# Placing the operands of a split fp32 matmul at multiples of 2048 bytes of the SBUF row

## The chip, the core and the metric

The kernel runs on one core of a Trainium2 chip. The metric is the device time of one execution in microseconds; lower is better. The engines are named as in the profile: PE (TensorE), PEld (TensorE's weight loads), DVE (VectorE), ACT (ScalarE), POOL (GpSimd) and SP (SyncE, which only issues DMAs here).

## The reference

Two transformer blocks are computed one after the other on a sequence of 512 tokens with a width of 1024, all in float32. Cut to what matters:

```python
def first_block(x, ...):                       # two layers
    for l in range(2):
        z = rms_norm(x, g_mix_norm[l]) @ w_in[l]
        # latent attention of 4 heads | a gating unit | moving averages, each normed and joined
        x = x + mix @ w_out[l]
        h = rms_norm(x, g_ffn_norm[l])
        x = x + (silu(h @ w_gate[l]) * (h @ w_up[l])) @ w_down[l]      # hidden width 2816

def second_block(h, p, ...):                   # two layers
    for i in range(2):
        # layer 0: gated short convolution; layer 1: dilated attention, 3 groups of 8 heads
        h = h + mixer(rmsnorm(h, norm_mix[i]))
        h = h + square(relu(rmsnorm(h, norm_mlp[i]) @ w_up[i])) @ w_down[i]   # hidden width 4096
        h = h + sigmoid(rmsnorm(h, norm_ple[i]) @ w_gate[i]) * (p[i] @ w_proj[i])
    return rmsnorm(h, norm_final)
```

## The kernel before

Activations are kept transposed: the channel is the partition, the 512 tokens lie along the row. The residual is `x_res`, eight tiles of 128 x 512. A product of two float32 matrices is made of three matmuls on a single-pass type (fp32r): each operand is split into a high part, which that type holds exactly, and a low part, the rest, and high x high, high x low and low x high are added up in PSUM. This is `triple`, lines 437 to 441; most of the kernel's matmuls come from its three lines. The exact fp32 matmuls (norm sums, transposes, attention scores and values) don't go through it.

The weights come as 216 slabs of 128 x 2048 floats, in the order in which they are used. SP fetches slab n into one half of `w_stage` as soon as GpSimd has split the slab before it in that half. GpSimd (`split`, lines 376 to 382) writes `w_high` (L379, a rounding copy) and then `w_low` (L381, the subtraction), each with two halves, after TensorE has finished the slab two before. A slab holds 16 blocks of 128 x 128, so 48 matmuls of 512 columns. Where weights are the stationary operand, a block of 512 bytes of the row is loaded and a 2048-byte activation tile is moved through it; for the values of the attentions and for the gating unit the roles are exchanged, and 512 or 256 columns of weights are moved.

The phases are mix, ffn, mix, ffn, conv, mlp, ple, attn, mlp, ple and a last norm (`ORDER`). At the start of each, ScalarE writes `x_high` from the residual (L970) and VectorE `x_low` (L1280). The hidden activations of ffn and mlp are split in the same manner: ScalarE writes the high part, VectorE the low one (L1322, L1343), and `down` (L515 to L544) moves them. In the mlp, VectorE scales a tile out of PSUM (L1337), squares it (L1340) and makes the low part (L1343).

All tensors of a partition's row are allotted one after the other, in the order of the `sb(...)` calls from L164 on, each rounded up to 32 bytes. Ahead of them lie the scratch for DMA descriptors, 16,384 bytes unless the program asks for less, and 128 bytes more. From this the places follow:

| tensors | bytes | first byte, past a multiple of 2048 |
|---|---|---|
| `x_res`, `x_high`, `x_low` | 16,384 each | 128 |
| `w_stage`, `w_high`, `w_low` | 16,384 each | 128 |
| `rstd`, `rope` | 2,048 and 4,096 | 128 |
| `ident`, `ones`, `cols_sb`, `stat` | 512, 512, 608, 96 | 128, 640, 1152, 1760 |
| `shared_area` (`ffn_*`, `mlp_*`, `ple_*`, `lat_*`, `mla_*`, `gate_pool_*`, `attn_*`, `qk*`, `v_tok*`) | 90,112 | 1856 |
| `work_area` (`work`, `scores2`, `probs_t2`) | 16,384 | 1856 |

Within the shared area every tensor that `triple` reads is a whole number of tiles of 2048 bytes, so all their tiles lie 1856 bytes past a multiple. In the mix phase `pool_in`, of 4,224 bytes, stands in the middle of the area, and `mla_out`, `pool_out`, `probs_t1` and `w_spat` lie behind it, 1984 past. Weight blocks begin every 512 bytes from 128 on, slices of 256 columns every 1024.

Of the kernel before, what the change touches and what calls it, by code (L numbers as in the profile page):

```python
# [24 lines left out]
F32 = mybir.dt.float32  # L25
# [7 lines left out]
P = 128  # L33
T = 512
# [12 lines left out]
EPS = 1e-6  # L47
MASKED = -1e30
TOK = T // P

COLUMNS = [("mix_norm", 16), ("ffn_norm", 16), ("q_lat", 4), ("kv_lat", 2), ("q_head", 2), ("k_head", 2),
# [4 lines left out]
N_COLUMNS = sum(n for _, n in COLUMNS)  # L57
# [40 lines left out]
SPLITS_MIX = 3 + DT  # L98
MIX_STEPS, MIX_HEADS, MIX_VALUES = 2 * HEADS * TOK, 2 * HEADS, 2 * HEADS
MIX_LOADS, FIRST_LOADS = 10, 2  # L100
# [52 lines left out]
def build(nc, a):  # L153

    ctx = ExitStack()
    with ctx:
        def sb(name, shape, dt=F32, stack=ctx):
            return stack.enter_context(nc.sbuf_tensor(name, shape, dt))
# [2 lines left out]
            return ctx.enter_context(nc.semaphore(name))  # L161

        x = sb("x_res", [P, DT, T])  # L164
        xh = sb("x_high", [P, DT, T], F32R)
        xl = sb("x_low", [P, DT, T], F32R)
        stage = sb("w_stage", [P, 2, SLAB])
        wh = sb("w_high", [P, 2, SLAB], F32R)
        wl = sb("w_low", [P, 2, SLAB], F32R)
        rstd = sb("rstd", [P, T])  # L170
        rope = sb("rope", [P, 2, T])
        ident = sb("ident", [P, P])
        ones = sb("ones", [P, P])
        cols = sb("cols_sb", [P, N_COLUMNS])
        stat = sb("stat", [P, 24])

        with ExitStack() as s:
            hh1 = sb("ffn_high", [P, FFN_TILES, T], F32R, s)
            hl1 = sb("ffn_low", [P, FFN_TILES, T], F32R, s)  # L180
# [6 lines left out]
        with ExitStack() as s:  # L187
            qk1 = sb("qk1", [P, 2 * HEADS, T], F32, s)
            vt1 = sb("v_tok1", [P, TOK, HEADS * V_HEAD], F32, s)
            lath = sb("lat_high", [P, 3, T], F32R, s)  # L190
            latl = sb("lat_low", [P, 3, T], F32R, s)
            kr = sb("k_rope", [P, T], F32, s)
            kr_positions = kr[:].bitcast(I32)
            vs = sb("sgu_v", [P, TOK, 256], F32, s)
            u = sb("sgu_u", [P, 2, T], F32, s)
            pin = sb("pool_in", [P, 2, 16 + T], F32, s)
            o1 = sb("mla_out", [P, HEADS, T], F32, s)
            po = sb("pool_out", [P, 2, T], F32, s)
            pt1 = sb("probs_t1", [P, TOK, T], F32, s)
            spat = sb("w_spat", [P, 4, P], F32, s)  # L200
            tri = sb("tri_sb", [P, P], F32, s)
            bsp = sb("b_spat", [P, 2, P], F32, s)
            gsv = sb("g_sgu", [P, 256], F32, s)
            wpool = sb("w_pool_sb", [P, 2, 64], F32, s)
            inv = sb("inv_count_sb", [P, 2, T], F32, s)
            diag = sb("diag_sb", [P, T], F32, s)
            pa = sb("window_a", [P, T + 16], F32, s)
            pb = sb("window_b", [P, T + 16], F32, s)
            nar = sb("token_cols", [P, 232], F32, s)
            areas = [nar]  # L210
        with ExitStack() as s:
            qk2 = sb("qk2", [P, 2 * GROUPS * BATCH_HEADS, T], F32, s)
            v2 = sb("v_tok2", [P, GROUPS, TOK, T], F32, s)
            o2 = sb("attn_out", [P, GHEADS, T], F32, s)
        with ExitStack() as s:

            mha = sb("mla_high", [P, HEADS, T], F32R, s)
            mla_ = sb("mla_low", [P, HEADS, T], F32R, s)
            sb("under_v_tok1", [P, TOK, HEADS * V_HEAD], F32, s)
            mhb = sb("gate_pool_high", [P, 4, T], F32R, s)  # L220
# [1603 lines left out]
```

## Time and profile before

| | |
|---|---|
| timed runs | 2793.62, 2794.19 and 2796.15 us; median 2794.19 |
| span of the profiled execution, first to last instruction | 2791.8 us |
| PE, share of the span with a matmul in flight | 95% |
| PEld, DVE, ACT, POOL | 77%, 54%, 17%, 53% |
| bytes moved by DMA | 236.70 MB, 85 GB/s over the span |
| slabs: DMAs of 1 MB each | 216 |

The profile gives no time of its own for the profiled execution beside its span; the span is 2.4 us below the median of the timed runs.
### The profile page before, as it was taken

The page shows a single profiled execution, that of the slowest core. Times are in us where ns is not written, and L with a number is a line of the kernel's source. Part 1 is how long each engine was busy: PE and PEld are TensorE (multiplying, and loading weights), DVE is VectorE, ACT ScalarE, POOL GpSimd, SP SyncE. Part 2 cuts the span into 40 slices and gives each one's busy share as a digit, 9 for nine tenths or more (in the row PEclk, how much of TensorE's full clock was granted, in tenths as well). Part 3 has the DMA queues.
Part 4 walks back from the last instruction along what each step waited for, and adds up shares of the span by engine and source line. Part 5 has one row for each costly group of instructions (what it writes and reads, how often), then busy time and mean ns, then how long its engine had stood idle before and what let it go on. Part 6 is the DMA issues. An engine that isn't in the chain of part 4 may idle for free.

```text
span 2791.8 us, 30840 instructions
## 1 busy us (share of the span) xinstructions
PE 2656.8 (95%) x11906; PEld 2156.5 (77%) x11906; DVE 1505.0 (54%) x1678; ACT 471.4 (17%) x777; POOL 1475.1 (53%) x465
## 2 busy tenths in 40 slices
PE   6889999999899999999999999898999999999997
PEld 6668888877588888787878887687788877878875
DVE  5766554047575440456751715895379357805526
ACT  3342111023421110101100102200310042100012
POOL 4526656544266665555655665455336514656652
PEclk9899999999899999999999999999999999999998
DMA  4102222231022322222322222222112302222221
GB/s 147 61 31 91 91 104 90 92 110 61 2 104 92 104 90 93 88 102 84 109 76 103 91 91 99 76 102 78 61 46 90 106 31 83 91 85 96 91 93 58
DMA packets 36891, 236.70 MB, mean 85 GB/s; under 512 B 4048, under 2 KB 5584, under 8 KB 9168
## 3 DMA queue, kind: packets, MB, share of 16 engines
q1 hardware_dynamic: 33456, 230.78, 24.0%
q10 hardware_dynamic: 3360, 4.85, 0.5%
q8 instruction: 56, 0.92, 0.1%
q14 instruction: 19, 0.16, 0.0%
HBM read 233.51 MB, written 2.10 MB: 84 GB/s over the span
## 4 chain that ended last, share of the span: by engine, by line
PE 82%; DVE 11%; issue 3%; ACT 2%; DMA 1%; POOL 0%; DVEq 0%; ACTq 0%; SPq 0%; POOLq 0%
PE psum L439 25%; PE psum L440 25%; PE psum L441 25%; DVE work L1340 3%; PE psum L887 2%; DVE work L1264 2%; DVE x_low L1280 1%; PE psum L871 1%; PE psum L649 1%; DVE work L1337 1%; PE psum L896 1%; ACT mlp_high L998 1%; DVE x_res L1384 1%; PE psum L759 1%; PE psum L775 1%
## 5 line engine op out<-in xcount | busy, mean ns | idle before, releaser
L379 POOL TENSOR_SCALAR w_high<-w_stage 128x2048 fp32r<-128x2048 f32 x216 | 418.5, 1937 | 1261.5 <-PE psum L441 1249.3
L381 POOL TENSOR_TENSOR w_low<-w_stage,w_high 128x2048 fp32r<-128x2048 f32 x216 | 1026.1, 4751 | 18.0
L439 PE MATMUL psum<-x_high,w_high 128*128 128x512 f32 x2048 | 807.3, 394 | 38.5 <-DVE x_low L1280 36.9
L440 PE MATMUL psum<-x_low,w_high 128*128 128x512 f32 x2048 | 801.0, 391 | 0.0
L441 PE MATMUL psum<-x_high,w_low 128*128 128x512 f32 x2048 | 800.8, 391 | 0.0
L439 PEld LDWEIGHTS psum<-x_high,w_high 128*128 128x128 f32 x2048 | 387.2, 189 | 123.9 <-issue 31.8
L440 PEld LDWEIGHTS psum<-x_low,w_high 128*128 128x128 f32 x2048 | 387.2, 189 | 82.9 <-issue 2.4
L441 PEld LDWEIGHTS psum<-x_high,w_low 128*128 128x128 f32 x2048 | 386.9, 189 | 81.3
L1304 DVE TENSOR_TENSOR x_res<-psum,x_res 128x512 f32<-128x512 f32 x64 | 47.0, 735 | 387.0 <-PE psum L441 387.0
L439 PE MATMUL psum<-mlp_high,w_high 128*128 (+1 forms) x576 | 230.2, 400 | 13.7 <-DVE work L1337 10.8
L440 PE MATMUL psum<-mlp_low,w_high 128*128 (+1 forms) x576 | 229.5, 398 | 0.0
L441 PE MATMUL psum<-mlp_high,w_low 128*128 (+1 forms) x576 | 229.4, 398 | 0.0
L970 ACT ACTIVATE x_high<-x_res,cols_sb 128x512 fp32r<-128x512 f32 x80 | 61.1, 771 | 545.1 <-DVE x_res L1304 545.1
L1343 DVE TENSOR_TENSOR mlp_low<-work,mlp_high 128x512 f32 x64 | 115.2, 1800 | 59.3 <-ACT mlp_high L998 59.3
L439 PEld LDWEIGHTS psum<-mlp_high,w_high 128*128 128x128 f32 x576 | 109.4, 190 | 42.5 <-DVE work L1337 12.6
L439 PE MATMUL psum<-ffn_high,w_high 128*128 (+1 forms) x352 | 138.7, 394 | 0.0
L440 PE MATMUL psum<-ffn_low,w_high 128*128 (+1 forms) x352 | 138.7, 394 | 0.0
L441 PE MATMUL psum<-ffn_high,w_low 128*128 (+1 forms) x352 | 138.7, 394 | 0.0
L1264 DVE TENSOR_TENSOR work<-work 128x512 f32<-128x512 f32 x87 | 134.2, 1543 | 2.6 <-ACT work L932 1.4
L1623 DVE TENSOR_TENSOR qk<-work 32x512 f32 x48 | 131.4, 2738 | 1.7
L441 PEld LDWEIGHTS psum<-mlp_high,w_low 128*128 128x128 f32 x576 | 109.3, 190 | 26.9
L440 PEld LDWEIGHTS psum<-mlp_low,w_high 128*128 128x128 f32 x576 | 109.4, 190 | 26.4
(240 smaller groups left out, 3172.3 us busy)
## 6 DMA issues: line engine op xcount, KB each, us to landing
w_stage<-in_wstream SPq DMA_DIRECT2D x216, 1024.0 KB, 4.9
x_res<-in_x SPq DMA_DIRECT2D x2, 1024.0 KB, 12.1
out_x<-attn_out SPq DMA_DIRECT2D x8, 256.0 KB, 2.1
inv_count_sb<-in_inv_count ACTq DMA_DIRECT2D x2, 512.0 KB, 8.9
ple_proj<-in_p ACTq DMA_DIRECT2D x2, 512.0 KB, 3.7
v_tok<-in_mask ACTq DMA_DIRECT2D x1, 576.0 KB, 3.8
w_spat<-in_spatial ACTq DMA_DIRECT2D x2, 256.0 KB, 5.3
diag_sb<-in_diag ACTq DMA_DIRECT2D x2, 256.0 KB, 9.6
```

Source lines behind the costliest of these rows:

```text
L379: pool.tensor_scalar(wh[:, s, :], stage[:, s, :], 1.0, 1.0, ALU.mult, ALU.mult).then_inc(high_written, 1)
L381: pool.tensor_tensor(wl[:, s, :], stage[:, s, :], wh[:, s, :].bitcast(F32), ALU.subtract) \
L439: pe.matmul(out, wa, ra, start=start, stop=False)
L440: pe.matmul(out, wa, rb, start=False, stop=False)
L441: return pe.matmul(out, wb, ra, start=False, stop=stop)
L887: last = pe.matmul(ps[:, b, r * P:(r + 1) * P], v, pt2[:, (n % 2) * 768 + kb * P:(n % 2) * 768 + (kb + 1) * P], start=kb == 0, stop=kb == 5)
L970: act.activation(dst, src, ACT.Copy, scale=gcol(p.gain + m)).then_inc(x_scaled, 1)
L1264: tt(W[:, ACC, :], W[:, ACC, :], src, ALU.add).then_inc(squares_added, 1)
L1304: tt(dst, src, dst, ALU.add).then_inc(drained[m], 1)
L1340: dve.scalar_tensor_tensor(out=W[:, 6 + m, :], in0=W[:, b, :], scalar=0.0, in1=W[:, b, :], op0=ALU.max, op1=ALU.mult).then_inc(product_rea ...
L1343: tt(hl2[:, bass.ds(i * 4 + b, 1), :].rearrange("p a t -> p (a t)"), W[:, 6 + m, :], hh2[:, bass.ds(i * 4 + b, 1), :].rearrange("p a t -> ...
L1623: tt(rotated, W[rows, 2 * m, :], W[rows, 2 * m + 1, :], ALU.add).then_inc(head_ready, 1)
```

## The change

The constants (`ident`, `ones`, `cols_sb`, `stat`) are allotted first, a padding that nobody reads fills up to byte 4096, and `rstd`, `rope`, the residual, its two parts and the slabs follow. The scratch for DMA descriptors is asked for at 1,024 bytes instead of 16,384, which makes room for the padding. As every tensor from there on up to `pool_in` is a whole number of 2048 bytes, the tiles of `x_high`, `x_low`, `w_high`, `w_low` and of the shared and the work area then begin at multiples of 2048, weight blocks at multiples of 512. In the mix phase `pool_in` goes behind the small constants, so that the tensors it pushed off move to multiples as well. No instruction, wait or transfer is added, removed or reordered.

```diff
+SCRATCH = 1024
+ROW_PAD = 4096 - (SCRATCH + 128) - 4 * (2 * P + 152 + 24)
...
+        ident = sb("ident", [P, P])
+        ones = sb("ones", [P, P])
+        cols = sb("cols_sb", [P, N_COLUMNS])
+        stat = sb("stat", [P, 24])
+        sb("up_to_a_row", [P, ROW_PAD // 4])
+        rstd = sb("rstd", [P, T])
+        rope = sb("rope", [P, 2, T])
         x = sb("x_res", [P, DT, T])
         xh = sb("x_high", [P, DT, T], F32R)
         xl = sb("x_low", [P, DT, T], F32R)
         stage = sb("w_stage", [P, 2, SLAB])
         wh = sb("w_high", [P, 2, SLAB], F32R)
         wl = sb("w_low", [P, 2, SLAB], F32R)
-        rstd = sb("rstd", [P, T])
-        rope = sb("rope", [P, 2, T])
-        ident = sb("ident", [P, P])
-        ones = sb("ones", [P, P])
-        cols = sb("cols_sb", [P, N_COLUMNS])
-        stat = sb("stat", [P, 24])
...
-            pin = sb("pool_in", [P, 2, 16 + T], F32, s)
             o1 = sb("mla_out", [P, HEADS, T], F32, s)
             po = sb("pool_out", [P, 2, T], F32, s)
             pt1 = sb("probs_t1", [P, TOK, T], F32, s)
             spat = sb("w_spat", [P, 4, P], F32, s)
+            inv = sb("inv_count_sb", [P, 2, T], F32, s)
+            diag = sb("diag_sb", [P, T], F32, s)
             tri = sb("tri_sb", [P, P], F32, s)
             bsp = sb("b_spat", [P, 2, P], F32, s)
             gsv = sb("g_sgu", [P, 256], F32, s)
             wpool = sb("w_pool_sb", [P, 2, 64], F32, s)
-            inv = sb("inv_count_sb", [P, 2, T], F32, s)
-            diag = sb("diag_sb", [P, T], F32, s)
+            pin = sb("pool_in", [P, 2, 16 + T], F32, s)
...
-    nc = bacc.Bacc("TRN2", target_bir_lowering=False, num_devices=1)
+    nc = bacc.Bacc("TRN2", target_bir_lowering=False, num_devices=1, dynamic_dma_scratch_size=SCRATCH)
```

## Rows read from the trace of the kernel before

**Rows 1.** The page, part 4: the chain that ended last, by engine and by line.

```profile
PE 82%; DVE 11%; issue 3%; ACT 2%; DMA 1%; POOL 0%; DVEq 0%; ACTq 0%; SPq 0%; POOLq 0%
PE psum L439 25%; PE psum L440 25%; PE psum L441 25%; DVE work L1340 3%; PE psum L887 2%; DVE work L1264 2%; DVE x_low L1280 1%; PE psum L871 1%; PE psum L649 1%; DVE work L1337 1%; PE psum L896 1%; ACT mlp_high L998 1%; DVE x_res L1384 1%; PE psum L759 1%; PE psum L775 1%
```

**Rows 2.** Groups by line, L439: out<-moving,stationary, shape, count | busy us, mean ns | idle before.

```profile
L439 PE MATMUL psum<-x_high,w_high 128*128 128x512 f32 x2048 | 807.3, 394 | 38.5 <-DVE x_low L1280 36.9
...
L439 PE MATMUL psum<-mlp_high,w_high 128*128 (+1 forms) x576 | 230.2, 400 | 13.7 <-DVE work L1337 10.8
...
L439 PE MATMUL psum<-ffn_high,w_high 128*128 (+1 forms) x352 | 138.7, 394 | 0.0
...
L439 PE MATMUL psum<-w_high,x_high 128*128 128x512 f32 x192 | 76.1, 396 | 8.8 <-DVE stat L1399 8.8
...
L439 PE MATMUL psum<-gate_pool_high,w_high 128*128 128x512 f32 x64 | 25.8, 404 | 3.1 <-DVE gate_pool_low L1551 3.1
...
L439 PE MATMUL psum<-w_high,x_high 128*128 128x256 f32 x64 | 20.6, 322 | 0.0
```

**Rows 3.** Three stretches: us, busy (count) of PE, PEld, DVE, ACT, POOL, PEclk, DMA.

```profile
300.00:400.00 100.00, 100.00 (x443) 82.80 (x442) 51.30 (x37) 17.81 (x23) 62.13 (x19) 1.00 0.27 94
470.00:570.00 100.00, 100.00 (x431) 80.12 (x430) 0.00 (x0) 0.00 (x0) 58.65 (x18) 1.00 0.27 93
2630.00:2710.00 80.00, 80.00 (x344) 64.11 (x344) 7.16 (x7) 2.80 (x5) 45.76 (x15) 1.00 0.28 93
```

**Rows 4.** Timeline of PE at half clock: start us, us, engine line op; four lie between.

```profile
595.81 0.63 PE L440 MATMUL psum<-x_low,w_high 128*128 128x512 f32 x1
...
597.94 0.63 PE L439 MATMUL psum<-x_high,w_high 128*128 128x512 f32 x1
```

**Rows 5.** Timeline of PE, weights as moving operand, 256 columns; five lie between.

```profile
62.34 0.28 PE L439 MATMUL psum<-w_high,x_high 128*128 128x256 f32 x1
...
63.06 0.28 PE L439 MATMUL psum<-w_high,x_high 128*128 128x256 f32 x1
```

**Rows 6.** Timeline of PE, exact fp32 matmuls of the attention; one row merges like ones.

```profile
2261.77 0.82 PE L896 MATMUL psum<-ident,scores 128*128 128x128 f32 x6
2262.43 1.02 PE L871 MATMUL psum<-qk 128*128 128x512 f32 x2
2263.29 0.38 PE L872 MATMUL psum<-qk 128*128 128x128 f32 x2
```

**Rows 7.** Timeline of two matmuls and their consumers, with the weight loads that follow.

```profile
285.98 0.39 PE L441 MATMUL psum<-x_high,w_low 128*128 128x512 f32 x1
285.98 0.19 PEld L439 LDWEIGHTS psum<-x_high,w_high 128*128 128x128 f32 x1
...
286.41 0.69 DVE L1316 TENSOR_TENSOR work<-psum,rstd 128x512 f32<-128x512 f32 x1 [3.51 <-PE psum L441]
...
1983.02 0.39 PE L441 MATMUL psum<-w_high,x_low 128*128 128x512 f32 x1
1983.45 0.69 ACT L1179 ACTIVATE v_tok<-psum,stat 128x512 f32<-128x512 f32 x1 [2.03 <-PE psum L441]
...
1984.20 0.19 PEld L871 LDWEIGHTS psum<-qk 128*128 128x128 f32 x1 [1.22 <-issue]
```

**Rows 8.** Spans and mean granted TensorE clock of the core.

```profile
core 0: 2791.8 us, clock 0.973
```

**Rows 9.** Timeline of POOL and DVE in an mlp up run, one slab.

```profile
2406.39 1.92 POOL L379 TENSOR_SCALAR w_high<-w_stage 128x2048 fp32r<-128x2048 f32 x1 [3.89 <-PE psum L441]
2408.39 4.92 POOL L381 TENSOR_TENSOR w_low<-w_stage,w_high 128x2048 fp32r<-128x2048 f32 x1
...
2405.30 0.69 DVE L1340 SCALAR_TENSOR_TENSOR work<-work 128x512 f32<-128x512 f32 x1
...
2409.48 4.38 DVE L1340 SCALAR_TENSOR_TENSOR work<-work 128x512 f32<-128x512 f32 x1
```

**Rows 10.** The page, part 6: the slab's DMA, count, size, us from issue to landing.

```profile
w_stage<-in_wstream SPq DMA_DIRECT2D x216, 1024.0 KB, 4.9
```

## Prediction

> **What bounds the kernel now.** The chain that ended last comes first: 82% of it is TensorE, 75% in the three lines of `triple`, and nothing else has over 3% in one line [rows 1]. So the end is set by how often TensorE can start one of these matmuls. The reader should next look at how many there are and of which operands, in the groups by line and shape [rows 2]; each row stands for three lines with equal counts, and `mla_high` and `attn_high` have the same counts as `gate_pool_high`. That makes, of 512 columns, 3 x 2048 with `x_high` and 3 x 192 with weights as the moving operand (6720 together, all moving operands 128 bytes past a multiple of 2048), and 3 x (352 + 576 + 3 x 64) = 3360 whose moving operand lies in the shared area, 1856 bytes past a multiple (the smaller groups there are left out). 3 x 64 = 192 move 256 columns of weights.
>
> A share of the chain doesn't say how far these are from their best, so the next view is the stretches of the long runs, all at the full granted clock [rows 3]. A matmul of 0.39 us touches a stretch if it starts in it or up to 0.39 us before, so the pitch from start to start is 100.39 / 443 = 226.6 ns with `x_high`, and 100.39 / 431 = 232.9 and 80.39 / 344 = 233.7 with `ffn_high` and `mlp_high`; I use 233.3. Two pitches for the same instruction, the same shape and the same clock: what differs is the operand's address.
>
> At half clock five `x_high` matmuls take 597.94 - 595.81 = 2.13 us, 426 ns each [rows 4], and half of this is 213.3 ns (512 columns at 2.4 GHz): the 13.3 ns of `x_high` and the 20.0 ns of the shared area exist at the full rate alone. Six matmuls of 256 columns take 63.06 - 62.34 = 0.72 us, 120 ns each against 106.7: 13.3 ns again, so the extra is paid once for an instruction and not by length [rows 5]. Exact fp32 matmuls, which take their elements at half the rate, hardly pay: six start-to-starts of L896 take 2262.43 - 2261.77 = 0.66 us, 110 ns where two passes of 128 columns are 106.7, and two records of L871 take 0.86 us where four passes of 512 are 0.853 [rows 6], the latter with `qk` from the shared area. Nor is it the weight load that runs beside the matmul: a consumer starts 286.41 - 285.98 = 0.43 us after a matmul with a load beside it and 1983.45 - 1983.02 = 0.43 us after one whose next load comes only at 1984.20 [rows 7].
>
> One rule gives all three numbers: 128 past a multiple of 2048 leaves 128 bytes, 32 elements, to the next multiple of 256; 1856 leaves 192 bytes, 48 elements; and 1024 further on, where every second weight slice of 256 columns starts, leaves 32 again. At 2.4 GHz 32 elements are 13.3 ns and 48 are 20.0 ns: as if the piece up to the next multiple went at half rate. This is inferred from three values; a multiple of 256 itself isn't among them.
>
> The Trainium skill bears on this in two places. The Trainium skill (TensorE: Matmul & The Clock Gate, section "Wait — 56ns, not 53.3ns?") puts back-to-back starts at N columns over 1.2 GHz when cold and at N over 2.4 GHz plus some 2.5 ns when warm, with no word on addresses; the half-clock rows agree, the full-clock rows stand 11 and 17 ns above it, and a change that reached it would end near 2660. The Trainium skill (SBUF — State Buffer, section "Who interferes with whom") holds that TensorE waits on nobody at SBUF; taken for the whole story it leaves the address no part, which is the no-change rival, and the two pitches of rows 3 speak against it.
>
> **The change, part by part.** Its core moves every moving operand of the split products, and every weight block, onto a multiple of 512 or 2048 bytes. No instruction is added or removed and no wait is moved; what changes is the price of 10,272 matmuls. No row shows such a matmul at a multiple at full rate, so its pitch is bounded: from below by 213.3 ns (half of rows 4), from above by 240.0 ns (the same rule with a whole piece of 64 elements, 26.7 ns, at half rate; the third rival below). Between them lie the 226.6 ns of now. I take 213.3 + 3 = 216.3 ns, the 3 ns being what each recorded matmul of L896 shows over its columns; it is nearest because the rule leaves no broken piece at a multiple. Then:
> - 6720 x (226.6 - 216.3) = 69.2 us
> - 3360 x (233.3 - 216.3) = 57.1 us
> - 192 x (120 - 109.7) = 2.0 us
>
> together 128.3 us. Matmuls at half clock gain nothing: the mean granted clock of 0.973 [rows 8] is 5.4% of the span, 151 us, at half; at 0.426 us each that holds at most 350 matmuls, and as much of it is waiting I take 170, so 2 us less.
>
> What hides the other engines. GpSimd splits each slab in 1.92 + 4.92 us and then waits 3.89 us for TensorE [rows 9]; a slab of 48 matmuls goes from 10.88 to 10.38 us, so that wait shrinks to 3.4 and still covers it. VectorE's L1340 takes 0.69 us alone and 4.38 when GpSimd's subtraction holds it [rows 9]; that is 3.7 us of slack in a slab, of which 0.5 goes. A slab's DMA needs 4.9 us [rows 10] of 10.38. If one of these covers were gone, what is missing from 0.5 us would come back on each slab of its stage (64 slabs hold the MLPs: at most 32 us). I take 2 us given back where stages begin and end, since the chain's VectorE part (11%, rows 1) isn't shortened.
>
> The rest costs nothing either way: no DMA is issued by GpSimd (the DMA issues of the page are SP's and ACT's, of which rows 10 show SP's main one), so nobody uses the smaller scratch; the padding is never read; `pool_in` gives up its place to become the odd one and feeds eight fp32 matmuls. The exact fp32 matmuls move too: 3 ns a record less or more on some 1,400 is 4 us, in both directions, taken as nothing. The DMA of a slab lands at another offset with the same 8,192 bytes a partition: nothing by the queue's slack.
>
> Sum: 128 - 2 - 2 = 124 us. The profiled span is 2791.8 us; the median of the timed runs is 2794.2, 2.4 us more, which the change doesn't touch. 2794 - 124 = 2670 us. With 213.3 ns it would be 6720 x 13.3 + 3360 x 20 + 192 x 13.3 = 159 us, 2635.
>
> **The rivals.**
> - Only the shared area gains. The 13.3 ns could belong to any single-pass fp32 matmul at full rate and only the additional 6.7 ns to an address off a multiple of 128 (1856 is, 128 isn't). Then the moved operands all run at 226.6: 3360 x 6.7 = 23 us, 2771. For it: the 256-column slices pay 13.3 too, wherever they start. Against it: the exact match of 32 and 48 elements.
> - The change doesn't do what it says: the pitch follows something else (which tile is read, not where), 2794. Against it: operands of different stages share a pitch when they share an offset.
> - Slower: the first piece of up to 256 bytes always goes at half rate, since the reader only gets ahead after it. Then a multiple is the worst place, 240.0 ns: 6720 x 13.4 + 3360 x 6.7 + 192 x 13.3 = 115 us, 2909. It fits all three values as well as my reading, and decides as soon as the mean pitch exceeds today's 228.8 ns. [...]
> - Part of the gain: a pitch of 218 to 224 ns or a cover that gives way, 2700 to 2760.
>
> **How the numbers follow.** The forecast has 0.50 (2635 to 2700 by its bounds), part of the gain 0.06, only the shared area 0.18, no change 0.12, slower 0.14. A change of 0.2%, 5.6 us, is about the least that a measurement of this kernel can tell from none. The range reaches from 2635 to 2800 and leaves out the slower case. Faster: 0.50 + 0.06 + 0.18 = 0.74; the same 0.12; slower 0.14.
>
> **What would show it.** In the changed profile, a stretch of 100 us of `x_high` should hold 464 matmuls, and so should one of `ffn_high`; 443 in both means the first rival, 418 the slower one. The 256-column matmuls should be 110 ns apart. GpSimd's wait for TensorE should shrink by 0.5 us a slab, VectorE's stay off the path. If the pitch is right and the time isn't, a cover is gone: TensorE would then wait for L381 or for a bank to be drained. The prediction is wrong altogether if the pitch doesn't depend on where the operand begins.

## The result, and the profile after

The changed kernel took 2776.55 us, median of four executions (2771.68, 2771.82, 2781.28 and 2784.05), against 2793.99 for the kernel before beside them: a ratio of 0.9939, 95% interval 0.992 to 0.9958. That is 17 us less, where 124 were forecast. The profiled execution is the one of 2781.28 us, with a span of 2779.5. Lines of the code stand one further down than before (L440 to L442 are `triple`'s).

The chain of the changed kernel, by engine and by line, to be read beside [rows 1]:

```profile
PE 79%; DVE 14%; issue 3%; ACT 2%; DMA 1%; POOL 0%; DVEq 0%; ACTq 0%; SPq 0%; POOLq 0%
PE psum L440 24%; PE psum L441 24%; PE psum L442 24%; DVE work L1341 3%; PE psum L888 2%; DVE work L1265 2%; DVE x_low L1281 1%; PE psum L872 1%; DVE work L1338 1%; PE psum L760 1%; PE psum L897 1%; ACT mlp_high L999 1%; DVE x_res L1385 1%; PE psum L776 1%; DVE qk L1395 1%
```

TensorE's part fell from 82 to 79% and VectorE's rose from 11 to 14%: something was given back there. First the pitch, though. Three stretches at full clock, with `x_high`, `ffn_high` and `mlp_high` as moving operand (length, PE busy and count, granted clock, DMA share, GB/s), answering [rows 3]:

```profile
300.00:400.00 100.00, 100.00 (x443) 1.00 0.27 94
470.00:570.00 100.00, 100.00 (x443) 1.00 0.28 101
2610.00:2690.00 80.00, 80.00 (x355) 1.00 0.30 105
```

The count with `x_high` is 443, as before; that with `ffn_high` went from 431 to 443, and that with `mlp_high` from 344 to 355 in 80 us. So there is now one pitch, 100.39 / 443 = 226.6 ns (80.39 / 355 = 226.5), and it is the lower of the two of before. That the shared area lost 6.7 ns a matmul is worth 3360 x 6.7, some 22 us, and two of the four executions show just that, 2794 - 22 = 2772. The matmuls of 256 columns didn't move either, against [rows 5] (six pitches of 120 ns):

```profile
62.18 0.28 PE L440 MATMUL psum<-w_high,x_high 128*128 128x256 f32 x1
...
62.90 0.28 PE L440 MATMUL psum<-w_high,x_high 128*128 128x256 f32 x1
```

The granted clock is where it was, 0.974 against 0.973 [rows 8], and in the mlp GpSimd still waits for TensorE between two slabs, 3.9 and 4.0 us here against 3.89 [rows 9]; an up run moves `x_high`, whose pitch stayed.

The other two executions are 10 and 12 us longer, and the profiled one, of 2781 us, is one of them. TensorE's waits in its second mixing layer (570 to 765 us) show most of it: what waits, for what, total, times and longest.

```profile
PE psum L789 <- DVE work L1577: 10.4, 4, 5.6
PE psum L722 <- DVE qk L1502: 6.9, 1, 6.9
PE psum L440 <- DVE x_low L1281: 3.7, 1, 3.7
```

The second of these isn't in the trace of the kernel before, whose largest waits there are 10.4 and 3.5 us on the other two lines. The first mixing layer (0 to 190 us) has it too, shorter, and again the kernel before has none there:

```profile
PE psum L722 <- DVE qk L1502: 2.6, 1, 2.6
```

What makes it is the subject of the last experiments.

### The profile page after: what moved, and what is told of

The parts are those of the page before. It is cut to its first block, busy times and chain, and to the rows that moved or that the text cites. A ratio compares the mean times of both kernels' runs of the same rounds, so it can differ in the third digit from the quotient of the medians.

```text
span 2779.5 us, 30840 instructions
## 1 busy us (share of the span) xinstructions
PE 2631.9 (95%) x11906; PEld 2155.3 (78%) x11906; DVE 1508.2 (54%) x1678; ACT 471.7 (17%) x777; POOL 1475.9 (53%) x465
## 3 DMA queue, kind: packets, MB, share of 16 engines
q10 hardware_dynamic: 3360, 4.85, 0.6%
## 4 chain that ended last, share of the span: by engine, by line
PE 79%; DVE 14%; issue 3%; ACT 2%; DMA 1%; POOL 0%; DVEq 0%; ACTq 0%; SPq 0%; POOLq 0%
PE psum L440 24%; PE psum L441 24%; PE psum L442 24%; DVE work L1341 3%; PE psum L888 2%; DVE work L1265 2%; DVE x_low L1281 1%; PE psum L872 1%; DVE work L1338 1%; PE psum L760 1%; PE psum L897 1%; ACT mlp_high L999 1%; DVE x_res L1385 1%; PE psum L776 1%; DVE qk L1395 1%
## 5 line engine op out<-in xcount | busy, mean ns | idle before, releaser
L382 POOL TENSOR_TENSOR w_low<-w_stage,w_high 128x2048 fp32r<-128x2048 f32 x216 | 1026.8, 4754 | 18.0
L440 PE MATMUL psum<-x_high,w_high 128*128 128x512 f32 x2048 | 806.9, 394 | 38.3 <-DVE x_low L1281 36.7
L442 PE MATMUL psum<-x_high,w_low 128*128 128x512 f32 x2048 | 800.1, 391 | 0.0
L440 PEld LDWEIGHTS psum<-x_high,w_high 128*128 128x128 f32 x2048 | 386.7, 189 | 124.5 <-issue 31.4
L442 PEld LDWEIGHTS psum<-x_high,w_low 128*128 128x128 f32 x2048 | 386.6, 189 | 80.4
L440 PE MATMUL psum<-mlp_high,w_high 128*128 (+1 forms) x576 | 227.0, 394 | 14.2 <-DVE work L1338 11.0
L442 PE MATMUL psum<-mlp_high,w_low 128*128 (+1 forms) x576 | 226.0, 392 | 0.0
L440 PEld LDWEIGHTS psum<-mlp_high,w_high 128*128 128x128 f32 x576 | 109.5, 190 | 39.1 <-DVE work L1338 12.7
L440 PE MATMUL psum<-ffn_high,w_high 128*128 (+1 forms) x352 | 136.9, 389 | 0.0
L442 PE MATMUL psum<-ffn_high,w_low 128*128 (+1 forms) x352 | 136.9, 389 | 0.0
L442 PEld LDWEIGHTS psum<-mlp_high,w_low 128*128 128x128 f32 x576 | 109.4, 190 | 23.0
```

What stands on the lines that cost most here:

```text
L382: pool.tensor_tensor(wl[:, s, :], stage[:, s, :], wh[:, s, :].bitcast(F32), ALU.subtract) \
L440: pe.matmul(out, wa, ra, start=start, stop=False)
L442: return pe.matmul(out, wb, ra, start=False, stop=stop)
```

## The experiments

**e1_micro: the pitch by itself.** TensorE alone, every address chosen; 40 matmuls to a line of the code:

```diff
+            for j in range(R): pe.matmul(ps[:, 0, :], st(0, j), mv(0, j), start=j == 0, stop=j == R - 1)
+            for j in range(R): pe.matmul(ps[:, 1, :], st(0, j), mv(64, j), start=j == 0, stop=j == R - 1)
...
+            for j in range(R): pe.matmul(ps[:, 3, :], st(64, j), mv(0, j), start=j == 0, stop=j == R - 1)
...
+            for j in range(R): pe.matmul(ps[:, 1, :], st(64, j), mv(64, j), start=j == 0, stop=j == R - 1)
```

`mv(m, j)` is a tile of the moving operand m bytes past a multiple of 2048, `st(w, j)` a weight block w bytes past one.

> Leaves out the whole computation: one TensorE queue of 41 x 40 matmuls and nothing beside them, one source line for each case, so that the pitch of a case is the distance between two lines' first starts over 40. Cases: moving operand 0 to 1856 bytes past a multiple of 2048 with the weights at 0; weights 32 to 1856 past with the moving operand at 0; both off; 128, 256, 384 and 512 columns; 128, 64 and 32 stationary columns; 64 rows; the same weight block or the same moving tile each time; bf16 and exact fp32. Theory A (multiples of 128: a moving operand off a multiple of 128 bytes costs 6.7 ns, and 13.3 ns belong to any such matmul at full rate): 226.7 ns at 0, 128, 256, 512, 1024; 233.3 at 4, 16, 32, 64, 192, 1856; the weights' address changes nothing. Theory B (the place within 2048 counts by itself): only 0 or a few places give 226.7. Theory C (the weights' address counts, or the two operands' offset against each other): 233.3 with the weights at 64 and the moving operand at 0, and 226.7 again with both at 64. Of the 13.3 ns: if the weight load makes them, 64 or 32 stationary columns or one weight block read again should give less, down to 213.3; if they belong to the data type, bf16 should stand nearer to 213.3 (216) and 256 columns of fp32 at 120; if they come with the address, no case at 0 should have them.

The timeline of PE, start and length in us. The pitch of a row is the distance to the next row's start over 40 (to some 0.3 ns, as the last matmul of a row belongs to the change over). L87 to L91 move operands at 0, 64, 128, 192 and 256 with the weights at 0; L98 and L101 have the weights at 64 and 192 with the moving operand at 0; L104 has both at 64; L122 and L123 are bf16 at 0 and 64, L124 and L125 exact fp32 at 0 and 64:

```profile
49.16 9.23 PE L87 MATMUL psum<-moving,weights 128*128 128x512 f32 x40
58.22 9.34 PE L88 MATMUL psum<-moving,weights 128*128 128x512 f32 x40
67.40 9.45 PE L89 MATMUL psum<-moving,weights 128*128 128x512 f32 x40
76.69 9.50 PE L90 MATMUL psum<-moving,weights 128*128 128x512 f32 x40
86.03 9.27 PE L91 MATMUL psum<-moving,weights 128*128 128x512 f32 x40
95.14 9.23 PE L92 MATMUL psum<-moving,weights 128*128 128x512 f32 x40
...
150.52 9.49 PE L98 MATMUL psum<-moving,weights 128*128 128x512 f32 x40
159.85 9.49 PE L99 MATMUL psum<-moving,weights 128*128 128x512 f32 x40
...
178.48 9.32 PE L101 MATMUL psum<-moving,weights 128*128 128x512 f32 x40
187.64 9.24 PE L102 MATMUL psum<-moving,weights 128*128 128x512 f32 x40
...
206.06 9.27 PE L104 MATMUL psum<-moving,weights 128*128 128x512 f32 x40
215.16 9.27 PE L105 MATMUL psum<-moving,weights 128*128 128x512 f32 x40
...
355.68 8.81 PE L122 MATMUL psum<-moving,weights 128*128 128x512 bf16 x40
364.32 8.80 PE L123 MATMUL psum<-moving,weights 128*128 128x512 bf16 x40
372.96 34.50 PE L124 MATMUL psum<-moving,weights 128*128 128x512 f32 x80
407.29 34.50 PE L125 MATMUL psum<-moving,weights 128*128 128x512 f32 x80
```

With the weights at 0 the moving operand costs 226.5, 229.5, 232.2, 233.5 and 227.8 ns at 0, 64, 128, 192 and 256. A multiple of 128 isn't good as such (128 costs 232.2), which ends theory A. Weights at 64 give (159.85 - 150.52) / 40 = 233.2, weights at 192 give 229.0, and both at 64 give 227.5. So what counts is the distance from the weights to the moving operand, modulo 256: 192 (64 on the weights' side) costs 233, 64 (192 on the weights' side) 229, and 0 some 227, wherever the two lie. That is theory C in its second form, the two operands' offset against each other, and both of its numbers came; that the offset counts modulo 256 and with its sign, no theory had.

No single-pass fp32 case of 512 columns took less than 226.5 ns, so the 13.3 ns stayed there, also with one weight block or one moving tile read over and over. bf16 takes (364.32 - 355.68) / 40 = 216.0 ns at either distance, exact fp32 (407.29 - 372.96) / 80 = 429.1 ns a record, and neither cares for these 64 bytes. The Trainium skill (TensorE: Matmul & The Clock Gate, section "Wait — 56ns, not 53.3ns?") has N over 2.4 GHz plus some 2.5 ns; the bf16 matmuls here agree (213.3 + 2.7), and so does a record of exact fp32 if its columns are counted twice (426.7 + 2.4), but the single-pass fp32 ones don't.

**e2_before_pad64: the whole gain for 64 bytes.** The kernel before, and nothing but this:

```diff
         stat = sb("stat", [P, 24])
+        sb("to_a_multiple_of_128", [P, 16])
```

> The kernel before with 64 unused bytes ahead of the shared area, which then begins 1920 bytes past a multiple of 2048 (15 x 128) in place of 1856; nothing else moves. Theory A (a multiple of 128 is enough): all split products at 226.7 ns, 3360 x 6.7 = 22 us less than before, 2771 to 2777 us, the same as the changed kernel. Theory B (it takes a multiple of 512 or 2048): no change, 2794 us, 233.3 ns from ffn_high and mlp_high.

Measured: 2780.6 us (2769.1 to 2781.7), ratio 0.9934, 0.9914 to 0.9954: the same as the whole change within the intervals, with four of its six executions near 2781. The stretch with `ffn_high` has 443 matmuls, with nothing on a multiple of 512 or 2048:

```profile
470.00:570.00 100.00, 100.00 (x443) 1.00 0.29 98
```

It fits theory A, and just as well the distance: 1920 - 128 = 1792 is 7 x 256.

**e3_after_shared64: the shared area 64 bytes off.**

```diff
         wl = sb("w_low", [P, 2, SLAB], F32R)
+        sb("off_by_64", [P, 16])
```

> The changed kernel with 64 unused bytes ahead of the shared area, so that only its tiles lie 64 bytes past a multiple of 2048; the constants stay first, and the scratch small. Theory A: 233.3 ns again for the tiles of the shared area, 226.7 for x_high, +22 us against the changed kernel, 2794 to 2799 us: the whole gain is the place of the shared area within 128 bytes. Rival (the gain came from the order of the constants, the scratch or the DMA's landing): 2772 to 2781 us, as the changed kernel.

Measured: 2776.9 us (2773.0 to 2788.1). Theory A wanted 233.3 ns and 2794 to 2799; the stretch with `ffn_high` holds 438, 100.39 / 438 = 229.2 ns:

```profile
470.00:570.00 100.00, 100.00 (x438) 1.00 0.29 100
```

That is the 229 of e1_micro for a distance of 64, not the 233 of the kernel before for one of 192, though both addresses are 64 past a multiple of 128. The time alone would have spoken for the rival on record (order, scratch, landing), and wrongly: only the count tells.

**e4_after_again: the changed kernel once more.**

> The changed kernel as it is, once more, for its spread: its runs so far lie at 2771.7 and 2784. If the spread goes with the granted clock in the mixing layers, the profiled run's distance from 2771.4 should show there, and the dense stages should take the same time to 0.2 us as in the first profile. With every split product at 226.7 ns and nothing given back, 2771.4 us is the floor of its runs.

Measured: 2771.3 us (2769.3 to 2781.7), ratio 0.9926, 0.9906 to 0.9946. Of its ten executions here and above, six lie between 2769 and 2772 and four between 2779 and 2785. Its profiled execution is one of the short ones, with a span of 2769.2 us, and in it TensorE has no wait for `qk` at L722 in the second mixing layer. The stretch of the first feed-forward layer, 190 to 573 us, holds the same PE time to 0.01 us in both profiles.

**e5_after_x64 and e6_after_w64: the same 64 bytes on either side.** The moved operand alone, and the weights alone:

```diff
+        sb("off_by_64", [P, 16])
         xh = sb("x_high", [P, DT, T], F32R)
         xl = sb("x_low", [P, DT, T], F32R)
+        sb("back_to_a_row", [P, 496])
```

```diff
+        sb("off_by_64", [P, 16])
         wh = sb("w_high", [P, 2, SLAB], F32R)
         wl = sb("w_low", [P, 2, SLAB], F32R)
+        sb("back_to_a_row", [P, 496])
```

> The changed kernel with 64 unused bytes ahead of x_high and 1984 behind x_low: only these two lie 64 bytes past a multiple of 2048. Theory D (distance of the moving operand from the weights, modulo 256): 6144 matmuls with x moving at a distance of 64, 228.9 ns, 6144 x 2.2 = 13.6 us; 576 with x as the weights at 192, 233.3 ns, 3.8 us; together 17 us more than the changed kernel, 2788 to 2798 us. Rival A (the moving operand's own place in 128 bytes, 6.7 ns when off): 6144 x 6.7 = 41 us more, 2812 to 2822 us. The rival that only the shared area's place counts: as the changed kernel, 2770 to 2781 us.

> The changed kernel with 64 unused bytes ahead of w_high and 1984 behind w_low: every moving operand but the weights' own stays at a multiple of 2048, and only the weights lie 64 bytes past one. Theory D: 6144 + 3360 matmuls at a distance of -64, that is 192, 233.3 ns, 9504 x 6.67 = 63.4 us, and 576 with w moving at 64, 1.3 us: 65 us more than the changed kernel, 2835 to 2846 us, four times the cost of the same 64 bytes on x. Rival A (only the moving operand's place counts): 576 x 6.7 = 4 us more, 2774 to 2786 us.

Measured: 2790.7 us (2788.0 to 2795.9) with `x` off, within 2788 to 2798; and 2829.6 us (2828.0 to 2830.9) with the weights off, 1.28% slower than the kernel before (ratio 1.0128, 1.0111 to 1.0145), where every moving operand but the weights' own lies on a multiple of 2048. The stretch with `x_high` holds 438 with `x` off (229.2 ns), 431 with the weights off (232.9):

```profile
300.00:400.00 100.00, 100.00 (x438) 1.00 0.27 94
```

```profile
300.00:400.00 100.00, 100.00 (x431) 1.00 0.27 93
```

The weights' place, which a reader would leave alone, costs 58 us against 2771; 65 were expected. By the starts of the phases the shortfall is in the two mixing layers: against e4_after_again the first takes 0.5 us longer and the second 1.8 us less, where the 384 matmuls of its eight slabs, at up to 6.7 ns each, would be up to 2.6 us more. TensorE waits for VectorE in these layers, so that a slower matmul need not show there; that this is the reason wasn't tested.

**e8_all64: everything 64 bytes off.**

```diff
+        sb("off_by_64", [P, 16])
         x = sb("x_res", [P, DT, T])
```

> The changed kernel with 64 unused bytes ahead of x_res: x, the weights and the shared area all lie 64 bytes past a multiple of 2048, at distances that are multiples of 256 from each other. Theory D: every split product at 226.7 ns, the same time as the changed kernel, 2769 to 2782 us, with nothing left on a multiple of 2048. Rival A: 233.3 ns for all moving operands, (6720 + 3360) x 6.7 = 67 us more, 2838 to 2849 us.

Measured: 2773.6 us (2771.7 to 2780.7), ratio 0.9926, 0.9909 to 0.9942, as the changed kernel, and at the same pitch:

```profile
470.00:570.00 100.00, 100.00 (x443) 1.00 0.29 102
```

The multiples of 2048 as such are worth nothing; the distance accounts for the gain.

**e7_micro2 and e9_micro3: the distance in steps, and the 13.3 ns.** The same bench with other cases, of these forms:

```diff
+            for j in range(R): pe.matmul(ps[:, 1, 0:256], st(0, j), mv(192, j, n=256), start=j == 0, stop=j == R - 1)
+            for j in range(R): pe.matmul(ps[:, 7, :], st(0, j, ws=4, step=2), mv(0, j), start=j == 0, stop=j == R - 1)
+            for j in range(R): pe.matmul(ps[0:64, 1, :], st(0, j, cols=64), mv(16, j), start=j == 0, stop=j == R - 1)
```

> Leaves out the whole computation, as e1_micro did: 40 TensorE matmuls to a source line. The first such run gave 226.7 ns where moving operand and weights lie equally far past a multiple of 256 bytes, and 229 to 237 otherwise. Here the distance between them goes from 0 to 240 bytes in steps of 16 (and 8, 248, 252) at 512 columns, and from 0 to 224 in steps of 32 at 256 columns; then 448 and 320 columns, weights read with a step of 2 or 4 elements, 32 rows, and a moving operand in two pieces of 256 columns. Theory D (the distance modulo 256 sets the pitch, with its least value at 0): 0 gives 226.7, 64 228.9, 128 232.3, 192 233.3, no distance below 226.7, and 256 columns show the same differences around 120 ns. Rival E (the distance only shifts how the reads of moving operand and next weights fall together, and 0 is no optimum): some distance below 226.7 at 512 columns, and another order at 256 columns (64 gave 117.8 there). Of the 13.3 ns: 448 and 320 columns 200.0 and 146.7 if they are paid once per matmul; weights with a step of 2 or 4 elements more, if they come from reading the next weights beside the moving operand, the same if not.

> Leaves out the whole computation, as the two before it: 40 TensorE matmuls of 512 columns to a source line, now with 64, 32 and 96 stationary columns at distances of 0 to 240 bytes from moving operand to weights, then 128 stationary columns at 228 to 244, and a moving operand read as its even and then its odd columns. The open question is the 13.3 ns that no distance took off 128 stationary columns. Theory F (they are two stalls of 6.67 ns that the next weights' 512 bytes cost the moving operand's reads): half the weights, 256 bytes, meet it about once, so that some distance gives 220.0 ns at 64 stationary columns, and 32 columns go to 213.3 to 220; 96 lie between. Theory G (they belong to every matmul of this data type at the full rate, whatever is loaded): no distance below 226.7 at 64, 32 or 96 columns. At 228 to 244 neither expects less than 226.7. Even and odd columns: F at least 226.7, since the operand's bytes are passed over twice; G 226.7.

At 512 columns the distances from 16 to 224 in steps of 16 gave 229 to 235 ns, and none less than 226.7. At 240 bytes it was (196.90 - 187.83) / 40 = 226.8 ns in e7_micro2 and (381.55 - 372.10) / 40 = 236.3 in e9_micro3, so something beside the distance counts as well, and what it is stays open. A distance of 0 gave 226.5 to 228.0, but for two rows of e1_micro (230.0 and 237.3) whose first matmul follows matmuls of another kind and is late. The rows (e7_micro2: L106 at a distance of 240; L116 of 256 columns at 192; L118 and L119 of 448 columns at 0 and 64):

```profile
187.83 9.23 PE L106 MATMUL psum<-moving,weights 128*128 128x512 f32 x40
196.90 9.50 PE L107 MATMUL psum<-moving,weights 128*128 128x512 f32 x40
...
253.29 4.70 PE L116 MATMUL psum<-moving,weights 128*128 128x256 f32 x40
257.83 4.89 PE L117 MATMUL psum<-moving,weights 128*128 128x256 f32 x40
262.56 8.43 PE L118 MATMUL psum<-moving,weights 128*128 128x448 f32 x40
270.83 8.16 PE L119 MATMUL psum<-moving,weights 128*128 128x448 f32 x40
278.83 6.02 PE L120 MATMUL psum<-moving,weights 128*128 128x320 f32 x40
```

At 256 columns a distance of 192 is the best, 4.54 / 40 = 113.5 ns against 120 at 0; at 448 columns 64 is better than 0, 200.0 against 206.8 (13.3 and 20.1 ns above 448 columns at 2.4 GHz); 320 columns took 146.5 at both. So theory D holds for 512 columns and not for the others, where 0 is no optimum, as rival E had it; E's other forecast, less than 226.7 ns somewhere at 512 columns, failed. The extra isn't a fixed 13.3 ns. Weights read with a step of 2 or 4 elements cost 233.3 and 235.0 ns at distance 0, in place of 226.7; by the expectation that speaks for the reading of the next weights as the cause, but doesn't show it. The last cases of e7_micro2 (32 rows, and two pieces of 256 columns) ran in part at half clock and say nothing. Then the number of weights (e9_micro3, 64 stationary columns at a distance of 16 in L92; L126 is 128 columns at 240, L128 the operand in even and then odd columns):

```profile
58.37 9.23 PE L92 MATMUL psum<-moving,weights 128*64 128x512 f32 x40
67.44 9.40 PE L93 MATMUL psum<-moving,weights 128*64 128x512 f32 x40
...
372.10 9.62 PE L126 MATMUL psum<-moving,weights 128*128 128x512 f32 x40
381.55 9.76 PE L127 MATMUL psum<-moving,weights 128*128 128x512 f32 x40
391.15 18.21 PE L128 MATMUL psum<-moving,weights 128*128 128x512 f32 x40
409.18 18.32 PE L129 MATMUL psum<-moving,weights 128*128 128x512 f32 x40
```

64 columns at 16, 48, 112 and 208, and 96 columns at 32, gave 226.5 to 227.0 ns and none less; 32 columns 230.0 to 233.5. Half the weights don't bring 220, so theory F falls. Theory G's forecast held, for 512 columns: some 226.7 ns is the least that they took in any case tried. Its reason, a price on every matmul of this type, isn't shown, since 256 columns at 192 pay half of it (113.5 - 106.7 = 6.8 ns). Even and odd columns of the same tile take twice as long, 451 ns, where theory G had 226.7 ns and theory F at least that, and neither a doubling.

**e10_split_later, e11_split_later2 and e12_split_later_again: the other 10 us.** First what precedes the wait at L722 in the changed kernel's profile (VectorE, GpSimd and TensorE in the second mixing layer):

```profile
651.60 4.98 DVE L1395 TENSOR_TENSOR qk<-qk,rope 32x512 f32<-32x512 f32 x1
...
659.21 7.43 DVE L1494 COPY probs_t<-token_cols 128x256 f32<-128x256 f32 x8
...
651.11 4.92 POOL L382 TENSOR_TENSOR w_low<-w_stage,w_high 128x2048 fp32r<-128x2048 f32 x1
...
662.02 4.54 POOL L382 TENSOR_TENSOR w_low<-w_stage,w_high 128x2048 fp32r<-128x2048 f32 x1
...
668.58 0.71 PE L722 MATMUL psum<-ident,probs_t 128*96 128x128 f32 x2 [6.89 <-DVE qk L1502]
```

VectorE's multiplication L1395 takes 0.68 us otherwise, its eight copies L1494 take 1.44 in the traces of before and of e4_after_again. Here each lies beside a subtraction of GpSimd, L382, as L1340 does in [rows 9]. The same lines in e4_after_again, this kernel in a short execution:

```profile
646.07 0.68 DVE L1395 TENSOR_TENSOR qk<-qk,rope 32x512 f32<-32x512 f32 x1
...
655.45 1.44 DVE L1494 COPY probs_t<-token_cols 128x256 f32<-128x256 f32 x8
...
650.82 4.57 POOL L382 TENSOR_TENSOR w_low<-w_stage,w_high 128x2048 fp32r<-128x2048 f32 x1
```

GpSimd starts a split when TensorE has finished a slab. In the long execution two subtractions meet VectorE's chain ahead of L722, and TensorE then stands for 6.9 us; in the short one and in the kernel before only one does. What differs between these two executions of one kernel is where TensorE's granted clock falls. It is full in the long one up to the sixth slab's split, at 649.11 us, and half in the short one ahead of its own, at 648.84 (granted clock: third number from the right; the long one first):

```profile
644.00:651.00 7.00, 7.00 (x38) 5.55 (x37) 6.71 (x11) 3.43 (x6) 1.89 (x1) 1.00 0.00 0
644.00:651.00 7.00, 7.00 (x21) 5.37 (x21) 5.22 (x13) 3.52 (x5) 2.08 (x2) 0.50 0.00 0
```

At full clock TensorE finishes the slab sooner after GpSimd's last split: GpSimd waits 13.4 to 13.5 us for it there in the four profiles with the wait of 6.9 us (the changed kernel, e2, e3 and e8), and 16.5 to 17.5 us, with the clock at half on the way, in before, e4 and e5, which have no such wait. e6, with 13.5 us, waits 0.8 at that place: its copies are done before the next subtraction begins. So the fall of the clock goes with the collision, as in the first half of rival I below, and faster matmuls alone don't explain it. Nor are long executions new: of the 46 of the kernel before that were run beside these kernels, four lie between 2801 and 2805 us, while of the twenty of the changed kernel, e2 and e8, nine lie between 2779 and 2785. None of the four was profiled, and why the faster kernels have so many more wasn't tested.

The edit lets the sixth slab's split wait for the last turned head (the second kernel also has the seventh wait for `factors_ready`):

```diff
-                    split_run(at, p.slab + 8)
+                    split_run(at, p.slab + 5)
+                    pool.wait_ge(head_ready, HEADS * (p.layer + 1))
+                    for n in (5, 6, 7):
+                        one(p.slab + n)
                     at = p.slab + 8
```

> The changed kernel with one wait more on GpSimd in each mixing layer: the sixth slab's split begins only when VectorE has turned the last head (head_ready). In the profiles of 2779 to 2780 us VectorE's L1395 took 4.98 us in place of 0.68 and the eight copies of L1494 7.43 in place of 1.44, both beside GpSimd's subtraction, and TensorE then waited 6.9 us for VectorE at L722; in the one of 2769.2 us neither is there. Theory H (the matmuls, once faster, let GpSimd start a slab's split earlier, into VectorE's chain, and this costs some executions 7 to 10 us): no wait of TensorE at L722, and nearly all runs between 2767 and 2774 us, median at or below 2771. Rival I (the runs differ by where the granted clock falls, and the collision only goes with it): runs at 2771 and at 2780 as before, median 2771 to 2781. Rival J (TensorE then waits for the later slab): 2 to 6 us more, 2773 to 2785 us, with a wait for w_low of GpSimd in the mixing layers.

> As e10_split_later, and the seventh slab's split also waits until VectorE has made the copies of L1494 (factors_ready). Theory H: as e10_split_later or 1 us better where the copies still met the seventh subtraction there, 2767 to 2773 us. Rival J is more likely here: if the seventh slab comes late, TensorE waits for its w_low and the time is 2773 to 2785 us. Rival I: runs at 2771 and 2780 as before.

> e10_split_later as it is, once more, since in its profiled execution the added wait was over before TensorE released the slab, and so didn't act. Theory H: the executions stay between 2765 and 2773 us, none at 2779 to 2784, where the changed kernel without the wait has 4 of 10; and where VectorE is late in the profiled one, GpSimd's split of the sixth slab is released by VectorE, L1396's line, and the copies take 1.4 us. Rival I (the five executions at 2766 to 2770 were chance): about two in five near 2780 again.

Measured: 2769.7 us (2765.7 to 2770.2), ratio 0.9911, 0.9897 to 0.9924; with the second wait too 2770.4 us (2767.4 to 2771.5), ratio 0.9918, 0.9905 to 0.9932; and the first once more 2768.2 us (2765.8 to 2771.2), ratio 0.9907, 0.989 to 0.9923. All fourteen executions lie below 2772, where four of ten lay near 2780 without the wait; the changed kernel wasn't run again beside them. GpSimd in the first mixing layer of e12_split_later_again shows the added wait at work (in brackets the idle time before, and what ended it), and that nothing comes too late, for the next slab is again released by TensorE:

```profile
89.17 1.93 POOL L380 TENSOR_SCALAR w_high<-w_stage 128x2048 fp32r<-128x2048 f32 x1 [16.34 <-DVE qk L1399]
...
97.56 1.90 POOL L380 TENSOR_SCALAR w_high<-w_stage 128x2048 fp32r<-128x2048 f32 x1 [1.77 <-PE psum L445]
```

VectorE releases that split in all three profiles, and TensorE's wait of 2.6 us at L722, which the changed kernel's profile has in this layer, is gone in all three. In the second mixing layer it is TensorE that releases the split last (e12_split_later_again):

```profile
645.60 1.92 POOL L380 TENSOR_SCALAR w_high<-w_stage 128x2048 fp32r<-128x2048 f32 x1 [16.33 <-PE psum L445]
```

The wait for TensorE is 16.3 to 17.5 us there in the three profiles, as in the executions without the wait of 6.9 us, so that none was to be expected there without the edit either. What is shown is thus the first layer's 2.6 us by traces, and the rest by the times alone. Theory H's forecast held and J's didn't: TensorE's wait for `w_low` in the second mixing layer is 1.7 us, as in e4_after_again. Rival I's forecast, executions near 2780 again, failed fourteen times, but its reading of the clock agrees with the traces; whether the added wait prevents the collision in the second layer, or moves the clock's fall, stays open. The two edits can't be told apart by time; e10_split_later is 23 to 26 us or 0.9% below the kernel before.

## Why the prediction was wrong

- **The bound and the counts: right.** The end is set by the pitch of 10,272 matmuls [rows 1 to 3]; 3360 x 6.7 = 22 us gives 2772, and the short executions lie at 2769 to 2772.
- **"One rule gives all three numbers": the step that failed.** It tied the extra time to where the moving operand lies in 256 bytes. The period was right and the reference wrong: e1_micro, e5 and e6 show the distance to the weights. In the kernel before the weights lie at 128, as `x_high` does, so that distance is 0 and the pitch 226.6; the shared area is 1856 - 128 = 1728 = 6 x 256 + 192 away, and 192 costs 233.3; the 256-column slices are at 0. The three numbers couldn't separate the two readings, since `w_high` and `w_low` never moved in that trace, and "what differs is the operand's address" left the second operand out. The weight load had been ruled out by two starts of consumers [rows 7], but both matmuls there have a distance of 0, and the rows are in steps of 10 ns, so that they couldn't have shown the 6.7 ns. The exact match of 32 and 48 elements was a coincidence: with both operands 64 bytes past a multiple the rule has 20 ns and e1_micro 227.5 - 213.3 = 14.2.
- **"Nearest because the rule leaves no broken piece": the taken 216.3 ns.** Measured 226.6. This is the term that carried the forecast: 69.2 us for `x_high` and the weights was 0, 57.1 for the shared area was 22, and the 2.0 of the 256 columns was 0. The value came from a rule rather than from the nearest row, which was the unchanged 226.6 itself.
- **"Paid once for an instruction": wrong.** It rested on one length, 256 columns at distance 0 [rows 5]; e7_micro2 has from 6.8 ns over the columns (256 of them at 192) to 20.1 (448 at 0) and more, by length and distance.
- **Half clock and exact fp32 [rows 4, 6]: right.** Both stayed as they were; exact fp32 takes 429.1 ns at the two distances of e1_micro.
- **What hides the other engines: right for the mlp, wrong for the mixing layers.** "2 us given back" was nothing in some executions and some 10 in others, 2.6 + 6.9 us of it in TensorE's waits at L722. The prediction had the very pair of engines, VectorE held by GpSimd's subtraction [rows 9], and looked at it only where there was slack. Its last sentence but one was the useful one: the pitch as a rival had it, the time not, so a cover was gone.
- **The rival "only the shared area gains": right in its time and its count** (2771, 443 in both stretches), **wrong in its rule**: e3 lies as far off a multiple of 128 as the kernel before and gains two thirds of the 6.7 ns. It deserved more than 0.18, since the 13.3 ns were in every row at full rate and no row had less. The slower rival falls by the 443.
- **No change, and what it was leaned on.** The two pitches spoke against it, and rightly. The Trainium skill (SBUF — State Buffer, section "Who interferes with whom") lists the reads of the moving operand and of the weights as independent and says that TensorE waits on nobody. For other engines nothing here speaks against it; for TensorE's own two reads the measurement does: with no other engine at work, e1_micro has 226.5 to 237 ns by their distance. The same section lets a VectorE instruction with two SBUF inputs contend with a GpSimd instruction that reads SBUF, and the 4.98 us of L1395 agree.

What stays open: why 512 columns of single-pass fp32 take 226.7 ns where bf16 takes 216, and by what mechanism the distance of the two operands counts. A matmul of this type without its weight load wasn't tried. Open too is what decides where the granted clock falls in the mixing layers, and with it which execution is a long one.

## What to carry to other kernels

Where a matmul has two operands in SBUF, an address effect may belong to their distance and not to either: before fitting a rule to one address, ask which address never varied in the trace, and vary both in a bench. For single-pass fp32 at 512 columns, place moving operands and weights a multiple of 256 bytes apart (0.7% here for 64 bytes of padding), and measure other lengths by themselves. Where the executions of one kernel fall into two groups, compare a profile of each before explaining either. After any speed-up of the bounding engine, look at who is released earlier by it, and whom that one holds.

## What the runs showed of the hardware

- Single-pass fp32, 512 columns, full clock: some 226.7 ns at a distance of 0 modulo 256 between moving operand and weights, 229 at 64, 232 at 128, 233.3 at 192, up to 240 at 244 bytes, and 226.8 or 236.3 at 240; 256 columns 113.5 to 120 ns; 448 columns 200.0 or 206.8. Reading every second column doubled the time, 451 ns.
- The distance has two signs: 64 bytes on the moving operand cost 229 ns, the same 64 bytes on the weights 233.
- A VectorE operation of 0.68 us took 4.98 beside GpSimd's subtraction of 4.92 us, and eight copies 7.43 us in place of 1.44. An execution that met this in both mixing layers was some 10 us longer, and in the changed kernel's two profiles it went with a granted clock of 1.00, not 0.50, ahead of the sixth slab's split.
